# The first turn of the expert routing split into its two heads

## The reference

```python
def block(xb):                                   # 128 tokens
    q = (xb @ w_query).reshape(T, 8, 2, 128)     # 8 heads, 2 sides
    scores = einsum('thpd,hpkd->thpk', q, sub_keys)      # 128 keys a side
    s_top, i_top = top_k(scores, 16)
    cand = s_top[:, :, 0, :, None] + s_top[:, :, 1, None, :]   # 16 x 16
    best, sel = top_k(cand.reshape(T, 8, 256), 16)
    idx = take_along_axis(cand_idx, sel)         # row of side 0 * 128 + row of side 1
    gate = softmax(best)
    act = gelu(einsum('thkd,td->thk', expert_down[idx], xb))
    return einsum('thk,thkd->td', gate * act, expert_up[idx])
```

## Time and profile before

| | |
|---|---|
| three runs | 2944.5, 2954.16, 2949.88 us; median 2949.88 |
| profiled execution | 2951.25 us, of which the span of the instructions is 2949.5 |
| busy in the span | PE 67%, DVE 65%, ACT 41%, POOL 39% |
| moved by DMA | 1181.83 MB, mean 401 GB/s |
| of that by gathers | 1073.81 MB, 88.9% of the DMA engines' time |
| mean granted clock of TensorE | 0.696 of full speed |

### The profile page before, as it was taken

One profiled execution on the slowest core, in us unless ns is written; L12 is line 12 of the kernel. 1 busy time (PEld: TensorE's weight loads), 2 busy tenths in 40 slices (PEclk: granted clock), 3 DMA queues, 4 the chain that ended last, 5 costly groups with the idle time before them and its releaser, 6 DMA issues.

```text
span 2949.5 us, 37543 instructions
## 1 busy us (share of the span) xinstructions
PE 1973.1 (67%) x12770; PEld 899.5 (30%) x12770; DVE 1914.2 (65%) x4707; ACT 1205.3 (41%) x3855; POOL 1148.5 (39%) x1032
## 2 busy tenths in 40 slices
PE   5788888887977466666665656566666666566553
PEld 4454453443534122232322312132222223232110
DVE  4776656665766366677576766677576766666544
ACT  1245444354454243444344443444344444444333
POOL 0043333333444244444444444444444444444332
PEclk9888987988988567666567557665666656666555
DMA  9599999999999999999999999999999999999997
GB/s 404 198 372 402 371 387 395 384 417 389 420 418 372 381 419 420 421 411 421 420 421 421 410 420 419 418 406 421 420 413 420 409 415 418 414 409 417 421 421 293
DMA packets 176213, 1181.83 MB, mean 401 GB/s; under 512 B 19731, under 2 KB 28947, under 8 KB 42774
## 3 DMA queue, kind: packets, MB, share of 16 engines
q0 software_dynamic: 147456, 1073.81, 88.9%
q1 hardware_dynamic: 28566, 105.63, 9.2%
HBM read 1170.98 MB, written 8.39 MB: 400 GB/s over the span
## 4 chain that ended last, share of the span: by engine, by line
DMA 52%; PE 23%; DVE 13%; ACT 7%; issue 3%; SPq 1%; POOL 1%; DVEq 0%; ACTq 0%; POOLq 0%
DMA work<-experts,expert_rows 40%; DMA weights<-experts,expert_rows 9%; PE ps_sum L750 7%; DVE work L1294 5%; PE ps_small L719 4%; PE ps_m L668 3%; PE ps_wide L694 2%; PE ps_m L632 2%; PE ps_m L612 2%; ACT weight L931 1%; DMA work<-w_ada 1%; ACT diag L936 1%; DMA h_next<-x_scratch 1%; DVE weights L1294 1%; ACT act_out L929 1%
## 5 line engine op out<-in xcount | busy, mean ns | idle before, releaser
L564 POOL DMA_INDIRECT work<-experts,expert_rows x836 | 933.0, 1116 | 1470.0 <-PE ps_sum L750 1295.1
L1294 DVE CUSTOM_DVE_ANT_0 work<-work 128x1024 f32<-128x1024 f32 x836 | 1020.7, 1223 | 666.8 <-DMA work<-experts,expert_rows 665.6
L750 PE MATMUL ps_sum<-work,diag 128*32 128x256 f32 x6688 | 750.0, 534 | 674.3 <-ACT diag L936 670.9
L929 ACT ACTIVATE act_out<-act_in 128x1 f32<-128x1 f32 x1024 | 207.5, 203 | 1228.1 <-DVE act_in L1294 1224.8
L750 PEld LDWEIGHTS ps_sum<-work,diag 128*32 128x32 f32 x6688 | 154.6, 127 | 1162.6 <-ACT diag L936 1095.3
L936 ACT ACTIVATE diag<-const,weight 128x32 f32<-128x32 f32 x1024 | 329.1, 321 | 33.6
L1294 DVE CUSTOM_DVE_ANT_0 weights<-weights,work 128x1024 f32<-128x1024 f32 x188 | 230.1, 1224 | 153.3 <-DMA weights<-experts,expert_rows 152.9
L564 POOL DMA_INDIRECT weights<-experts,expert_rows x188 | 212.5, 1130 | 299.6 <-PE ps_sum L750 289.7
L931 ACT ACTIVATE weight<-gate,act_out 128x1 f32<-128x1 f32 x1024 | 301.7, 295 | 33.2
L750 PE MATMUL ps_sum<-weights,diag 128*32 128x256 f32 x1504 | 176.1, 555 | 203.8 <-ACT diag L936 196.4
L694 PE MATMUL ps_wide<-h_cur,const 32*128 32x512 f32 x260 | 211.4, 904 | 0.8 <-ACT work L903 0.8
(11 more groups left out here) (159 smaller groups left out, 1717.6 us busy)
## 6 DMA issues: line engine op xcount, KB each, us to landing
work<-sides SPq DMA_DIRECT2D x68, 576.0 KB, 8.1
work<-w_ada SPq DMA_DIRECT2D x12, 2048.0 KB, 23.8
work<-experts,expert_rows POOLq DMA_INDIRECT x836, 16.2
weights<-sides SPq DMA_DIRECT2D x12, 576.0 KB, 36.8
weights<-w_in SPq DMA_DIRECT2D x3, 2048.0 KB, 17.8
x_buf<-x SPq DMA_DIRECT2D x8, 512.0 KB, 11.2
weights<-w_out SPq DMA_DIRECT2D x2, 2048.0 KB, 37.0
x_scratch<-h_buf SPq DMA_DIRECT2D x8, 512.0 KB, 7.8
```

What stands on the lines that cost most here:

```text
L564: nc.gpsimd.indirect_dma_start(ring[x.ring], None, experts, bass.IndirectOffsetOnAxis(ap=rows_flat[:, x.column:x.column + 1], axis=0),).th ...
L750: last = nc.tensor.matmul(ps_sum[quarter(c), x.group, :], diag[:, x.ring, :], ring[x.ring][:, D + c * QCOLS:D + (c + 1) * QCOLS], start=x. ...
L929: nc.scalar.activation(act_out[:, s:s + 1], act_in[:, s:s + 1], ACT.Gelu).then_inc(s_gelu, 1)
L1294: nc.vector.tensor_tensor_reduce(down, down, h2_spread[x.segment % 2], 1.0, 0.0, ALU.mult, ALU.add, act_in[:, x.g % TURN:x.g % TURN + 1]). ...
```

## The change

The two heads of turn 0 of tile 0 become two routings of their own (`ROUTINGS`): the 19 steps run for head 0 (sides 0 and 1) and its choices are moved and placed, then the same for head 1. All other turns stay one routing of two heads; their numbers go up by one. In tile 0 the first batch of 32 slots becomes two of 16, with 4 slots in each group, so the first 32 slots have eight segments of 4 slots, where they had four of 8. A segment that follows one of 4 slots has its spreads behind slots 1 and 2 of that one, where they stood behind 1 and 3. The moved choices of turn 1 go to slot 23, where they were at 21, as the bank is taken.

In the head, PE's order becomes: spread of segment 0, the transposes of tile 1, the rows of GATE2, `move_choices(0)`, side 0 of turn 1, the projection of V, `move_choices(1)`, sides 1, 2 and 3 of turn 1. ACT makes the exp of head 0 after the copies of the first spread, and that of head 1 after side 0 of turn 1. The copies of turn 1's scores wait for step 1 of routing 1. The diff, cut to its core:

```diff
@@ -79,7 +79,15 @@
     ROUTE_AT += [SLOTS * _t + s for s in (2, 28, 68, 94)][:2 if _t == TILES - 1 else 4]
 
 
-BATCHES = [((0,), (1,), (2,), (3,))] + [((0, 1), (2, 3))] * (TILES - 1)
+ROUTINGS = [(0, (0,)), (0, (1,))] + [(e, tuple(range(PAIR))) for e in range(1, TURNS)]
+HEAD_GATHERS = TOPK // QUADS
+
+BATCHES = [((0,), (1,), (2,), (3,), (4,))]
+BATCHES += [((PAIRS * t + 1, PAIRS * t + 2), (PAIRS * t + 3, PAIRS * t + 4)) for t in range(1, TILES)]
+
+
+def head_range(heads, each):
+    return slice(heads[0] * each, (heads[-1] + 1) * each)
 
 C_IDENT = 0
 C_QUADS = C_IDENT + P
@@ -123,16 +131,17 @@
 
     table, starts = [], []
     for t in range(TILES):
-        for n, turns in enumerate(BATCHES[t]):
+        for n, routings in enumerate(BATCHES[t]):
             for group in range(QUADS):
                 starts.append((len(table), t, group))
-                for q in turns:
-                    for i in range(GATHERS):
-                        x = Slot(len(table), turns, group, (group * PAIRS + q) * GATHERS + i, len(starts) - 1)
-                        x.first = n == 0 and group % 2 == 0 and q == turns[0] and i == 0
-                        x.last = n == len(BATCHES[t]) - 1 and q == turns[-1] and i == GATHERS - 1
-                        x.opens = group == 0 and q == turns[0] and i == 0
-                        table.append(x)
+                of_group = [(ROUTINGS[r][0] % PAIRS, i) for r in routings
+                            for i in range(GATHERS)[head_range(ROUTINGS[r][1], HEAD_GATHERS)]]
+                for m, (q, i) in enumerate(of_group):
+                    x = Slot(len(table), routings, group, (group * PAIRS + q) * GATHERS + i, len(starts) - 1)
+                    x.first = n == 0 and group % 2 == 0 and m == 0
+                    x.last = n == len(BATCHES[t]) - 1 and m == len(of_group) - 1
+                    x.opens = group == 0 and m == 0
+                    table.append(x)
     fills, last = [0] * RING, [None] * RING
     for x in table:
         fills[x.ring] += 1
@@ -166,20 +175,22 @@
 def wide_bank_uses():
 
 
-    uses = [(-5, ("turn", 0, 0)), (-4, ("turn", 0, 1)), (-3, ("copy", 0, 0)), (-2, ("copy", 0, 1)), (-1, ("moved", 0))]
+    uses = [(-6, ("turn", 0, 0)), (-5, ("turn", 0, 1)), (-4, ("copy", 0, 0)), (-3, ("copy", 0, 1))]
+    uses += [(r - 2, ("moved", r)) for r in range(2)]
     for k in range(1, len(SEGMENTS)):
-        uses += [(SEGMENTS[k - 1][0] + 1 + 2 * half, ("copy", k, half)) for half in range(2)]
+        step = 1 if SEGMENTS[k][0] - SEGMENTS[k - 1][0] <= HEAD_GATHERS else 2
+        uses += [(SEGMENTS[k - 1][0] + 1 + step * half, ("copy", k, half)) for half in range(2)]
     for t in range(1, TILES):
         uses += [(SLOTS * (t - 1) + PREP_AT[t - 1] + TURN_H2 + 2 * half, ("turn", t, half)) for half in range(2)]
         uses += [(SLOTS * t + PAIR_SUM_SLOT + END_LATER[t], ("pair", t - 1))]
     uses += [(SLOTS * TILES, ("pair", TILES - 1))]
-    taken = {g + i for g, _ in uses for i in range(2)}
+    taken = {g + i for g, _ in uses for i in range(2 if g >= TURN else 1)}
     for e in range(1, TURNS):
         g = ROUTE_AT[e] + MOVE_SLOT
-        while g in taken or g + 1 in taken:
+        while g in taken or (g + 1 in taken and g >= TURN):
             g += 1
         taken |= {g, g + 1}
-        uses += [(g, ("moved", e))]
+        uses += [(g, ("moved", e + 1))]
     uses.sort()
     return {what: n for n, (_, what) in enumerate(uses)}, {what: g for g, what in uses}
@@ -731,13 +742,16 @@
                     pe.wait_ge(s_mod1, 3)
                 nc.tensor.matmul(ps_s, q_t[:, n % 2, :], keys, start=True, stop=True).then_inc(s_score, 1)
 
-            def move_choices(e):
-
-                pe.wait_ge(s_route, ROUTE_STEPS * (e + 1))
-                pe.wait_ge(s_wide_sb, WIDE_USE["moved", e])
+            def move_choices(r):
+
+                pe.wait_ge(s_route, ROUTE_STEPS * (r + 1))
+                pe.wait_ge(s_wide_sb, WIDE_USE["moved", r])
                 own = chosen_own[:, :, :].rearrange("p g (e i j) -> p j (g e) i", e=2, j=QUADS)
+                moved = ps_moved.rearrange("p (x i) -> p x i", i=GATHERS)
+                part = head_range(ROUTINGS[r][1], HEAD_GATHERS)
                 for j in range(QUADS):
-                    last = nc.tensor.matmul(ps_moved[quarter(j), :], quad_rows, own[:, j, :, :], start=True, stop=True)
+                    last = nc.tensor.matmul(moved[quarter(j), :, part], quad_rows, own[:, j, :, part],
+                                            start=True, stop=True)
                 last.then_inc(s_wide_ps, 1)
 
             def add_expert(x):
@@ -794,13 +808,13 @@
             spread_h2(0, 1)
             mixer(TURN_H, 1)
             mod_rows(GATE2)
-            for b in range(2):
-                side(1, b)
-                scores(1, b)
+            move_choices(0)
+            side(1, 0)
+            scores(1, 0)
             for n in range(TURN_H + 1, MIX_HEAD):
                 mixer(n, 1)
-            move_choices(0)
-            for b in range(2, 4):
+            move_choices(1)
+            for b in range(1, 4):
                 side(1, b)
                 scores(1, b)
@@ -912,19 +926,20 @@
             def copy_score(e, b):
                 act.wait_ge(s_score, 4 * e + b + 1)
                 if e:
-                    act.wait_ge(s_route, ROUTE_STEPS * (e - 1) + 2)
+                    act.wait_ge(s_route, ROUTE_STEPS * e + 2)
                 nc.scalar.copy(score[:, b, :], ps_s).then_inc(s_score_sb, 1)
 
-            def exp_logits(e):
-                act.wait_ge(s_route, ROUTE_STEPS * e + 10)
-                nc.scalar.activation(expd[:, :], logits[:, :], ACT.Exp).then_inc(s_exp, 1)
+            def exp_logits(r):
+                part = head_range(ROUTINGS[r][1], TOPK)
+                act.wait_ge(s_route, ROUTE_STEPS * r + 10)
...
@@ -966,11 +981,12 @@
             copy_score(0, 3)
             copy_spread(0, 0)
             copy_spread(0, 1)
+            exp_logits(0)
             for n in range(SCALE_H + 1, MIX_HEAD):
                 mixer(n, 1)
             for b in range(4):
-                if b == 2:
-                    exp_logits(0)
+                if b == 1:
+                    exp_logits(1)
                 copy_query(1, b)
                 copy_score(1, b)
@@ -1190,65 +1206,69 @@
-            def route_step(n, e):
-
-                exp_v = expd[:, :].rearrange("p (h k) -> p h k", h=PAIR)
-                base = ROUTE_STEPS * e
+            def route_step(n, r):
+
+                e, heads = ROUTINGS[r]
+                part, flat = head_range(heads, 1), head_range(heads, TOPK)
+                own_sides = range(2 * heads[0], 2 * heads[-1] + 2)
+                exp_v = expd[:, :].rearrange("p (h k) -> p h k", h=PAIR)[:, part, :]
+                base = ROUTE_STEPS * r
                 if n == 0:
-                    dve.wait_ge(s_score_sb, 4 * (e + 1))
-                    for b in range(4):
+                    dve.wait_ge(s_score_sb, 4 * e + own_sides[-1] + 1)
+                    for b in own_sides:
                         last = nc.vector.max(top_s[:, b, 0:8], score[:, b, :])
                     last.then_inc(s_route, 1)
                     return
...
+                elif n == SPREAD_STEP:
+                    for e2 in range(2):
+                        last = nc.vector.tensor_tensor(
+                            chosen_own[:, :, e2 * TURN + flat.start:e2 * TURN + flat.stop],
+                            chosen[:, e2, flat].unsqueeze(1).to_broadcast([P, QUADS, TOPK]),
+                            own_group.unsqueeze(2).to_broadcast([P, QUADS, TOPK]), ALU.mult)
                 last.then_inc(s_route, 1)
 
-            def place_choices(e):
-                dve.wait_ge(s_wide_ps, WIDE_USE["moved", e] + 1)
+            def place_choices(r):
+                e, heads = ROUTINGS[r]
+                part = head_range(heads, HEAD_GATHERS)
+                dve.wait_ge(s_wide_ps, WIDE_USE["moved", r] + 1)
                 moved = ps_moved.rearrange("p (g e i) -> p e g i", g=QUADS, e=2)
-                columns = slice(e % PAIRS * GATHERS, (e % PAIRS + 1) * GATHERS)
-                nc.vector.tensor_copy(expert_rows[:, :, columns], moved[:, 0, :, :]).then_inc(s_placed, 1)
-                nc.vector.tensor_copy(gate[:, :, columns], moved[:, 1, :, :]).then_inc(s_wide_sb, 1)
+                columns = slice(e % PAIRS * GATHERS + part.start, e % PAIRS * GATHERS + part.stop)
+                nc.vector.tensor_copy(expert_rows[:, :, columns], moved[:, 0, :, part]).then_inc(s_placed, 1)
...
-            for n in range(ROUTE_STEPS):
-                route_step(n, 0)
-            place_choices(0)
+            for r in range(2):
+                for n in range(ROUTE_STEPS):
+                    route_step(n, r)
+                place_choices(r)
             gate2_rows()
```

(30 more changed lines are left out.)

39 lines of the change are left out of this document (20 added, 19 removed).

## The result

The changed kernel is slower by 0.42%: 2963.34 us median (2959.19 to 2970.24, seven runs) against 2952.66 (2944.5 to 2956.62, seven runs), ratio 1.0042, 95% interval 1.0028 to 1.0057. That is about 12 us by the ratio and 10.7 by the medians. The profiled execution took 2959.19 us, with a span of 2957.4, 7.9 more than the span of before; it is the fastest of its seven, so its trace shows the loss somewhat small. One run of the kernel before, 3035.97 us at a lower clock than its others, is left out of the ratios of the last three experiments.

A forecast was written before the change was run, and what follows sets the result against it. It took a chain of PE and DVE as the bound to about slot 24, then DMA. At add(24), 2.6 + 6.6 - 3.2 = +6.0 us, passed on in full from a median of 2949.88, gave 2956 us; range 2941 to 2967.

The forecast's parts named there:

- the likeliest case: Whole kernel: a difference from the kernel before within 0.3% (8.85 us), chance 0.69.
- rival B: Turn 0's slots: short segments throttle DVE, 1.4 us for each of three segments; 12.5 us slower in all, 2962 us, chance 0.22.
- Step 1: Head of tile 0: routing one head takes 9.4 us, so the first gather starts near 135.7 us, 12.7 us earlier.
- Step 2: Up to add(0): the ring fills, side 3's load lands in 7.2 us, PE stands 3.5 us; adds start 2.6 us later.
- rival C: Load of side 3: not late, landing in 3.8 us; +2.5 us, 2952.5 us, inside the forecast's case, whose chance is 0.58.
- Step 3: Slots 0 to 23: +6.6 us for more spread matmuls, -3.2 us for PE waits that go.
- the spreads: Slots 0 to 23: twelve spread matmuls instead of six, at 1.1 us of PE time each, +6.6 us.
- the early rows: Slots 0 to 23: six rows in the ring early remove PE waits that stem from DVE, -3.2 us.
- the two waits of PE: PE's waits for diag before add(4), 2.46 us, and add(7), 0.78 us, which were to go.
- PE's extra work is the price: Slots 0 to 23: the added spread matmuls cost +6.6 us on PE, busy for 96% of 200 to 240 us.
- Step 4: From add(24) to the end: DMA share is 1.01 and nothing refills the delay, so 6 us pass on in full.
- Rival A: From 150 us on: DMA is the bound, the head start survives; 7 us of gain, 2943 us, chance 0.20.

The follow-up runs named there:

- side 1 early: The first experiment: the changed kernel with side 1 of turn 1 ahead of the projection of V again; ratio 1.0017 to the kernel before.
- mended, gathers late: The "both mended" kernel, but POOL waits for both heads' choices before slot 0; ratio 1.0007 to the kernel before.
- both mended: The changed kernel with side 1 of turn 1 ahead of the projection of V and turn 0 in 8-slot segments; ratio 0.9980 to the kernel before.
- short segments alone: The kernel before with only turn 0's 32 slots cut into eight 4-slot segments with sixteen spreads, routing still of two heads; ratio 1.0039 to the kernel before.
- spreads doubled: The "both mended" kernel with each spread matmul of segments 1 to 4 done twice into the same bank; ratio 0.9994 to the kernel before.

## Why the prediction was right or wrong

The direction and the range (2941 to 2967) held. The size did not: +6 us was forecast, and 11 to 12 came, a ratio of 1.0042 where the likeliest case was to stay within 0.3% (the interval's lower end, 1.0028, just reaches into it). The rival B of the forecast, at 2962, is the one that came about, by the place where it was put.

**Step 1 held.** The first gather was issued at 134.17 instead of 135.7. The head of this execution stood 1.4 us earlier; against its own head the gather came 12.8 us earlier, and 12.7 was forecast. One head's routing took 9.9 us from its first step to the end of its last (122.74 to 132.65) instead of 9.4, which cost nothing, since PE's rows of GATE2 ended only then.

**Step 2 had the mechanism, and two terms were too small.** The load landed in 7.9 us, 7.2 was taken; PE stood for 4.74 us instead of 3.5, and rival C, a load that is not late, did not come about. What the forecast left out is that PE comes out of such a wait at the lower clock:

```profile
154.00:156.00 2.00, 1.37 (x6) 1.40 (x7) 0.00 (x0) 0.00 (x0) 0.00 (x0) 0.50 0.88 358
```

Side 3's 16 matmuls took 3.75 us where side 2's took 2.02, and from their start to add(0) it was 7.55 us instead of 5.45. So against its own head add(0) moved by +5.9 instead of +2.6: 1.2 more by the stall and 2.1 more by what stood behind it. (The +4.5 between the two traces has the 1.4 us of the earlier head in it.) The first experiment shows that this is the late load, and that it passes to the end (7.1 us at add(0) counted from the spread, some 7 in the ratio).

The Trainium skill ("DMA: Bandwidth & Descriptors", section "Queues, rings and completion order") says that each DMA engine goes round-robin between the queues that have work. The forecast had read this as half the rate for the load and had put an estimate of 5.2 us beside its own. The trace decides against half the rate: 7.9 us behind the gathers, and 3.4 with none. From 148 to 151 us, beginning 1.4 us after its issue, the gathers' queue (q0) and SP's (q1) moved, in packets, MB and share of the engines:

```profile
q0 software_dynamic: 152, 1.07, 84.9%
q1 hardware_dynamic: 41, 0.19, 15.2%
```

**Step 3 had nearly the right sum from terms that were both too small, which is luck.** Forecast were +6.6 for the spreads and -3.2 for the early rows, +3.4; slots 0 to 23 became 4.4 us longer. The runs have slots 0 to 23 for long and for short segments, with late and with early rows:

| | rows late | rows early |
|---|---|---|
| segments of 8 | 79.5 (before), 78.8 (mended, gathers late) | 71.3 (both mended) |
| segments of 4 | 88.3 (short segments alone) | 83.9 (side 1 early) |

- The early rows: -7.5 with segments of 8, and -4.4 with segments of 4, instead of -3.2. The second pair differs in the split of the routing and in PE's order too, which by the upper left field are worth some 0.7.
- The short segments: +8.8 with late rows, +12.6 with early ones, instead of +6.6.

The two terms are not independent, since short segments take away a part of what early rows give. Added in one order the errors are +2.2 and -1.2, in the other +6.0 and -5.0 (with the 0.7); in both they cancel to +1.0.

Why the early rows are worth more than the two waits of PE that the forecast had counted, the chain shows. The forecast had said that before slot 24 the DMA is not what ends last. In the trace of before the chain does run over a DMA there, from 152.23 us until DVE has the row of slot 3, and from then to 206 us it is nearly all DVE:

```profile
152.23 13.61 DMA work<-experts,expert_rows
```

The kernel "mended, gathers late" has the same piece, 13.46 us long, and "both mended" has none. The first nine slots (add(0) to add(9)) of the one and of the other, columns as in the earlier trace rows:

```profile
156.42:186.96 30.54, 26.74 (x197) 18.83 (x197) 25.76 (x69) 11.67 (x33) 11.03 (x9) 0.85 1.01 420
```

```profile
156.81:180.74 23.93, 23.93 (x197) 17.12 (x197) 23.41 (x66) 11.54 (x34) 12.18 (x9) 0.93 0.89 318
```

With early rows PE never stands in these slots, and 6.6 of the 7.5 us are made in them. PE's wait before add(13), of which the forecast had said that it stays, is 2.5 us in both kernels; add(13) comes earlier by what was won before it.

The 12.6 us of the short segments (71.3 to 83.9) can be taken apart. 4.3 are PE time (spreads doubled). 7.1 come back when the same spreads stand one slot earlier (83.9 to 76.8): 4.9 of them are there by add(13), and 2.2 come behind it, where PE, after its longer wait, has one slot more at the lower clock. The two add up to 11.4; the last 1.2 us are not told apart.

So the failed step is "PE's extra work is the price": it carried the forecast's sum, while the hold on DVE was put in a rival at 0.22. That rival's mechanism was right, that a dot(4k+4) can't run ahead of PE any more. Its size, 1.4 us for each of three segments, was 4.2 against some 7 here.

**Step 4 held.** The 8.9 us at add(24) became 9.7 at slot 48 and 8.0 at the last gather. The 13.6 at slot 35 comes behind the two spreads of slots 24 to 31 and DVE's wait before dot(28), and 4 us of it are taken back by slot 42, where DMA is the bound again, as was said of those spreads.

**Rival A** was wrong for the changed kernel, but not in itself: the mended one has its head start and keeps 6 us. The DMA engines' share of 0.95 to 1.01 was the wrong reason; it is the row of slot 3, and with it DVE's chain, that comes early.

## What to carry to other kernels

An earlier start of a queue of transfers is worth what the first consumer can use of it: look at the ring's depth, at what stands before the first release, and at which loads of that stretch share the DMA engines with it. Cutting work into shorter segments cost less here by its instructions (4.3 us) than by the distance that is left between producing a segment's operand and using it (7.1 us); look whether the producer can move ahead with it. One slot was tried, no further. When a sum comes out right, test its terms apart, and in both states of the other: here each term was too small, and their errors hid each other. And before two traces are compared by their times, find a point up to which the programs are the same, and count from there.

## What the runs showed of the hardware

A wait of PE can be paid twice. After the 4.9 us before add(13) in the changed kernel the next groups ran at the lower level, 1.2 GHz: the spread took 2.07 us instead of 1.12, an add 1.08 instead of 0.64. The kernel before has this too, behind a wait of 3.2 us there; what the change adds is that two spreads fall into the stretch, and add(13) to add(16) takes 12.3 us instead of 10.7. With the spreads one slot earlier the wait is 2.6 us and the stretch takes 10.0. The granted clock from 200 to 220 us was 0.69 before, 0.66 in the changed kernel and 0.83 in the one with the spreads earlier (rows in this order):

```profile
200.00:220.00 20.00, 18.40 (x88) 9.57 (x89) 17.04 (x39) 9.68 (x29) 7.09 (x6) 0.69 0.96 368
```

```profile
200.00:220.00 20.00, 14.64 (x71) 7.26 (x72) 18.80 (x44) 9.60 (x26) 5.99 (x6) 0.66 0.75 267
```

```profile
200.00:220.00 20.00, 16.46 (x84) 7.39 (x88) 15.29 (x40) 9.84 (x27) 8.36 (x7) 0.83 0.98 390
```

A load of 576 KB on SP's queue landed in 3.4 to 3.8 us on idle DMA engines and in 5.7 to 9.5 us with gathers of 1 MB in flight (the earlier trace rows and the three loads after).
